# Stick-breaking layer of a two-block transformer kernel: normalisation after the product, additions in PSUM, results in two parts

## The chip, the cores and the metric

The kernel runs on one core of a Trainium2 chip. The metric is the device time of one execution in microseconds. Engines are called PE (TensorE), DVE (VectorE), ACT (ScalarE), POOL (GpSimd) and SP (SyncE, which issues the loads of weights).

## The reference, cut to what matters

The program computes two blocks of two layers each, on 512 tokens (528 with 16 meta tokens in the second block) of width 1024. The change is to the mixer of the second block's odd layer: a product to q, k and v, stick-breaking attention with 16 heads of 64, a product back.

```python
def stick_breaking(q, k, v):                 # 128-query blocks
    for i in range(L // BLOCK):
        s, e = i * BLOCK, (i + 1) * BLOCK
        z = einsum('bqhd,bkhd->bhqk', q[:, s:e], k[:, :e]) * scale      # scale = 1/8
        mask = (arange(e)[None, :] < arange(s, e)[:, None])[None, None]
        log_1m = where(mask, log_sigmoid(-z), 0.0)
        rest = cumsum(log_1m, axis=3, reverse=True) - log_1m
        a = where(mask, exp(log_sigmoid(z) + rest), 0.0)
        outs.append(einsum('bhqk,bkhd->bqhd', a, v[:, :e]))

def odd_mixer(h, w_in, w_out):               # h is rmsnorm(h, norm_mix[1])
    q, k, v = split(h @ w_in, 3, axis=-1)
    return stick_breaking(heads(q), heads(k), heads(v)).reshape(Bsz, L, C_W) @ w_out
```

With softplus(z) = -log_sigmoid(-z), a weight is exp(z minus the sum of the softplus of all keys from this one on that the query may see).

## The kernel before, in words

Activations are held transposed, features on the 128 partitions and the 528 tokens along the free dimension. Every large product is made in three passes over operands split into a high part (`hi`, rounded to fp32r) and a low part (`lo`, the rest): hi by hi, hi by lo, lo by hi. Weights come in panels of 1 MB (`Panels`, line 208): SP loads a panel two ahead (line 233), ACT makes its high part (line 244), DVE its low part (line 252), into two buffers each.

The odd layer (`odd_layer`, line 1971) is a row of blocks of code; all engines meet at the end of each block.

1. `normed_parts` (line 1673): the tails of two buffers are cleared on POOL, then `norm_stage` (line 527) squares the eight chunks of `hT` on ACT, adds them up with one-column matmuls (line 564), takes the root, spreads 1/rms over the partitions with matmuls of a diagonal (line 570), multiplies on DVE (line 600), and splits the result into two parts.
2. `product_stage` (line 333) makes q and k in 16 tiles of 48 matmuls (`wide_tile`, line 312, two matmuls of 264 columns to each stationary matrix), then v in 20 tiles of 24 matmuls of 256 columns (`row_tile`, line 324). ACT and DVE take finished tiles by turns (line 1032).
3. `stick_stage` (line 1735). Keys are on the partitions, queries along the free dimension. Key block t needs the queries from 128t on, so a head has 528 + 400 + 272 + 144 + 16 = 1360 columns. The work is in steps of one head each, written as a loop of four heads a turn (`over_steps`), and each engine works on several heads at different stages in one step. For a new head PE makes scores key block by key block (`score`, line 1920) into two PSUM tiles, from which ACT copies them, scaled by 1/8, to `z` in SBUF (line 1818). DVE bounds a copy (line 1897), ACT takes Exp and Ln (lines 1830, 1832), DVE takes the larger of that and z (line 1872), masks it (line 1876), masks z (line 1880), ACT and POOL split the softplus in two parts (lines 1825, 1851). For the head before, PE adds up the softplus over the keys into one PSUM tile, `sums`, from the last key block to the first (`add_up`, line 1934): after each block DVE subtracts the sums so far from z (line 1890), and PE may go on only when that is done (`normed`). ACT takes Exp of the finished z (line 1811) and PE mixes v with it (line 1959). ACT and POOL also stage the two parts of q and k for every pair of heads (lines 1805 to 1844), and POOL the head's part of v (line 1857).
4. `split_stage` (line 683) splits the result `y` into two parts on ACT (line 690) and DVE (line 697).
5. `product_stage` makes the product back, 8 tiles of 48 matmuls, which DVE adds to `hT` (line 1648).

The feed-forward layers (`ffn_layer`, line 2108) already do without step 1. `Parts` (line 2082) splits `hT` times the gain in two parts; `Rstd` (line 2010) works out 1/rms at the same time (squares on ACT, sums on POOL, two groups of small matmuls), and the tiles are multiplied by it as they leave PSUM.

## Time and profile before

| | |
|---|---|
| time, median of 3 runs | 3418.18 us (3412.99 to 3421.04) |
| time of the profiled execution | 3412.95 us |
| its span, first to last instruction | 3411.2 us |
| PE busy | 2788.7 us (82%) |
| DVE, ACT, POOL busy | 1237.9, 1033.5, 499.4 us |
| mean granted clock of PE | 0.796 of full speed |

The span is 1.75 us less than the time of the same execution. Stages follow one another with little overlap, so a stage's stretch of the span is its share of the time. "Busy" of PE says that matmuls were in flight, at either of its two clocks.

### The profile page before, as it was taken

Reading aid. Unit: us, or ns where it says so; the run is one execution under the profiler, and the core shown is the slowest. Engines: PE = TensorE matmul, PEld = TensorE weight load, DVE = VectorE, ACT = ScalarE, POOL = GpSimd, SP = SyncE. Lnnn points to the kernel's source line nnn. Section 1 sums busy time; section 2 is a strip of 40 time slices with the busy share of each in tenths; the row PEclk is TensorE's granted clock in tenths of the full one; section 3 lists DMA queues with packets and bytes.
Section 4 is the critical chain, followed back from the end, with each engine's and each line's share of the span. In section 5 each row is a group of like instructions: output and inputs, shape, how many; then the busy total and the mean of one; then the engine's idle time right before and its main releaser. Section 6 shows DMA issues by size and latency. Waiting matters only on the chain. (4 is left out here: it accounts for less than half of the span.)

```text
span 3411.2 us, 45824 instructions
## 1 busy us (share of the span) xinstructions
PE 2788.7 (82%) x18417; PEld 2577.8 (76%) x18417; DVE 1237.9 (36%) x2097; ACT 1033.5 (30%) x1535; POOL 499.4 (15%) x369
## 2 busy tenths in 40 slices
PE   5984978895697796669658989999896777799998
PEld 4973758894577696569447989999895554799998
DVE  1236232325423323331642344342323444343442
ACT  3233332225232210221323243231214444232232
POOL 0002100001100101200123033030002222032130
PEclk6996557897557698779555799999896666899998
DMA  3210001220001121011000223332220000232321
GB/s 105 87 50 6 1 3 50 87 75 6 1 1 52 38 75 42 19 50 56 33 1 0 68 75 84 97 91 77 71 79 1 0 0 0 62 83 77 105 74 59
DMA packets 232723, 165.44 MB, mean 48 GB/s; under 512 B 7439, under 2 KB 229513, under 8 KB 232421
## 3 DMA queue, kind: packets, MB, share of 16 engines
q1 hardware_dynamic: 232548, 162.91, 16.0%
q8 instruction: 134, 2.20, 0.3%
q14 instruction: 41, 0.33, 0.0%
HBM read 160.76 MB, written 2.14 MB: 48 GB/s over the span
## 5 line engine op out<-in xcount | busy, mean ns | idle before, releaser
L252 DVE TENSOR_TENSOR panel_lo<-panel_raw,panel_hi 128x2048 fp32r<-128x2048 f32 (+2 forms) x155 | 335.1, 2162 | 361.6 <-ACT panel_hi L244 361.6
L244 ACT ACTIVATE panel_hi<-panel_raw 128x2048 fp32r<-128x2048 f32 (+2 forms) x155 | 276.4, 1783 | 597.1 <-PE product L319 464.7
L328 PE MATMUL product<-panel_hi,normed_hi 128*128 128x256 f32 (+1 forms) x1336 | 378.7, 283 | 10.2 <-PEq L541 10.2
L328 PE MATMUL product<-panel_hi,normed_lo 128*128 128x256 f32 (+1 forms) x1336 | 378.6, 283 | 0.0
L328 PE MATMUL product<-panel_lo,normed_hi 128*128 128x256 f32 (+1 forms) x1336 | 378.6, 283 | 0.0
L319 PE MATMUL product<-scaled_hi,panel_hi 128*128 128x264 f32 x1408 | 289.9, 287 | 19.6 <-DVE scaled_lo L2097 12.5
L319 PE MATMUL product<-scaled_lo,panel_hi 128*128 128x264 f32 x1408 | 289.7, 287 | 0.0
L319 PE MATMUL product<-scaled_hi,panel_lo 128*128 128x264 f32 x1408 | 289.5, 287 | 0.0
L328 PEld LDWEIGHTS product<-panel_hi,normed_hi 128*128 128x128 f32 x1336 | 258.1, 193 | 10.2 <-issue 10.2
L328 PEld LDWEIGHTS product<-panel_hi,normed_lo 128*128 128x128 f32 x1336 | 258.2, 193 | 0.0
L328 PEld LDWEIGHTS product<-panel_lo,normed_hi 128*128 128x128 f32 x1336 | 258.1, 193 | 0.0
L319 PEld LDWEIGHTS product<-scaled_hi,panel_hi 128*128 128x128 f32 x1408 | 221.9, 191 | 20.9 <-DVE panel_lo L252 18.8
L319 PEld LDWEIGHTS product<-scaled_lo,panel_hi 128*128 128x128 f32 x1408 | 221.1, 191 | 0.0
L319 PEld LDWEIGHTS product<-scaled_hi,panel_lo 128*128 128x128 f32 x1408 | 220.9, 191 | 0.0
L319 PE MATMUL product<-normed_hi,panel_hi 128*128 128x264 f32 (+1 forms) x720 | 148.8, 288 | 40.2 <-PEq L541 40.2
L902 PE MATMUL scores<-panel_hi 64*128 64x512 f32 (+2 forms) x176 | 96.6, 670 | 93.8 <-POOL panel_lo L861 84.8
L564 PE MATMUL sums<-ones,squares 128*128 128x1 f32 x560 | 115.5, 343 | 63.5 <-ACT squares L549 63.5
L564 PEld LDWEIGHTS sums<-ones,squares 128*128 128x128 f32 x560 | 114.8, 319 | 66.1 <-ACT squares L549 66.1
L933 PE MATMUL mixed<-rows,e_turned 128*128 x768 | 151.3, 369 | 0.0
L933 PEld LDWEIGHTS mixed<-rows,e_turned 128*128 128x128 f32 x768 | 150.3, 291 | 0.1
L319 PE MATMUL product<-normed_lo,panel_hi 128*128 128x264 f32 (+1 forms) x720 | 148.1, 288 | 0.0
L319 PE MATMUL product<-normed_hi,panel_lo 128*128 128x264 f32 (+1 forms) x720 | 147.9, 287 | 0.0
(278 smaller groups left out, 5508.2 us busy)
## 6 DMA issues: line engine op xcount, KB each, us to landing
panel_raw<-in_w_in_dram SPq DMA_DIRECT2D x26, 1024.0 KB, 5.3
panel_raw<-in_ffn_w_gate_dram SPq DMA_DIRECT2D x44, 512.0 KB, 4.0
panel_raw<-in_ffn_w_up_dram SPq DMA_DIRECT2D x44, 512.0 KB, 5.3
panel_raw<-in_ffn_w_down_dram SPq DMA_DIRECT2D x32, 704.0 KB, 4.6
panel_raw<-in_even_w_in_dram SPq DMA_DIRECT2D x21, 1024.0 KB, 5.2
panel_raw<-in_odd_w_in_dram SPq DMA_DIRECT2D x12, 1024.0 KB, 5.1
panel_raw<-in_w_out_dram SPq DMA_DIRECT2D x8, 1024.0 KB, 5.1
panel_raw<-in_even_w_out_dram SPq DMA_DIRECT2D x8, 768.0 KB, 4.8
```

Source lines behind the costliest of these rows:

```text
L244: act.activation(c.hi[g % 2][:, 0:used], c.raw[g % 2][:, 0:used], ACT.Copy).then_inc(c.hi_made.sem, 1)
L252: dve.tensor_tensor(c.lo[g % 2][:, 0:used], c.raw[g % 2][:, 0:used], c.hi[g % 2][:, 0:used].bitcast(F32), ALU.subtract).then_inc(c.lo_made ...
L319: done = pe.matmul(out[:, b, 0:v - u], weight(w, k), a[:, k, u:v], start=(k == 0 and x == 0), stop=(k == chunks - 1 and x == 2))
L328: done = pe.matmul(out[:, 0, 0:v - u], a[:, k, t * P:(t + 1) * P], w[:, k, u:v], start=(k == 0 and x == 0), stop=(k == chunks - 1 and x == 2))
L564: done = pe.matmul(sums[:, t:t + 1], squares[k % 2][:, t * P:(t + 1) * P], c.ones[:, 0:1], start=(k == 0 and t == 0), stop=(k == KD - 1), ...
L902: done = pe.matmul(scores[a % s_ring][:, u:v], q[j][rows, b * P:(b + 1) * P], k[j][rows, u:v], start=(w == 0), stop=(w == 2))
L933: done = pe.matmul(mixed[n % 2][:, 0:d_v], e_turned[n % 2][0:rows, t, :], v_of(i, j, m, t)[0:rows], start=(t == 0), stop=(t == tiles - 1))
```

## The change

- The odd layer no longer calls `normed_parts`. A new block `odd_into` uses `Parts` and `Rstd`, makes v first (ACT multiplies a tile by 1/rms of its rows as it copies it), then q and k by turns; DVE multiplies their tiles by the spread 1/rms, ACT and POOL write the two parts, of all heads, to `q_hi`, `q_lo`, `k_hi`, `k_lo`. There is no staging for each head any more.
- A last block of fewer than 128 tokens is now one of 128 that begins at 400 (`block_starts`), so nothing is padded or cleared, in `Rstd` of the feed-forward layers too.
- In the new `stick_stage` z stays in PSUM, in three banks, for two heads at a time. PE makes the scores and adds the mask to them, by a matmul of the identity with the mask. Softplus is taken from it, and PE then adds minus 8 times its sums to the same banks. For each key block that takes the blocks after it too, so there is no running `sums` tile and no subtraction on DVE. ACT takes Exp from PSUM with scale 1/8.
- A head is handled in two parts (bank 0, 512 columns; banks 1 and 2, 864 columns), all written out without a loop. One activation table is loaded at the start of the stage.
- DVE writes the mixed values straight into `q_hi` and `q_lo`, from which the product back reads. `split_stage` is gone.

Core of the diff (constants, counters and signatures are left out):

```diff
-    into = Product(c, KD, 256, [Segment(8, columns(w_in, 0, 256), T_tiles(), take_into(lambda: cell.qk)),
-                             Segment(4, columns(w_in, 2048, 256), N_tiles(NB2), take_rows_into(lambda: cell.v))])
+    into = Product(c, KD, 256, [Segment(4, columns(w_in, 2048, 256), [("N", u) for u in block_starts(TOK)], None),
+                                Segment(8, load_qk, T_tiles(), None)])
...
+                for i in range(n_v):
+                    w_hi, w_lo = panels.split(pe, first + i)
+                    for t, at in enumerate(starts):
+                        n = i * len(starts) + t
+                        if n == RING:
+                            norm.pe_sums(pe, sums)
+                            norm.pe_spread(pe, sums)
+                        pe.wait_ge(c.v_taken.sem, c.v_taken.at(n - RING + 1))
+                        row_tile(...)
...
+                act.preload_act_table_set("natural_log_exp_and_others")
...
+                for h in range(H + 1):
+                    if h < H:
+                        x = soft[h % 2]
+                        for part in range(2):
+                            act.wait_ge(c.z_bounded.sem, c.z_bounded.at(2 * h + part + 1))
+                            act.activation(Stick.of(x, part), Stick.of(x, part), ACT.Exp).then_inc(c.z_exp.sem, 1)
+                        for part in range(2):
+                            act.wait_ge(c.z_exp.sem, c.z_exp.at(2 * h + part + 1))
+                            act.activation(Stick.of(x, part), Stick.of(x, part), ACT.Ln, bias=c.ones[:, 0:1]).then_inc(c.z_log.sem, 1)
+                    if h >= 1:
+                        for part in range(2):
+                            act.wait_ge(c.rest_ready.sem, c.rest_ready.at(2 * (h - 1) + part + 1))
+                            act.activation(Stick.of(weight[(h - 1) % 2], part), Stick.banks(z[(h - 1) % 2], part), ACT.Exp,
+                                           scale=0.125).then_inc(c.stick_made.sem, 1)
+                    if h < H:
+                        for part in range(2):
+                            act.wait_ge(c.plus_made.sem, c.plus_made.at(2 * h + part + 1))
+                            act.activation(Stick.of(plus_hi[h % 2], part), Stick.of(x, part), ACT.Copy).then_inc(c.plus_hi.sem, 1)
...
+                for h in range(H):
+                    add_up(h)
+                    if h >= 1:
+                        mix(h - 1)
+                    if h + 2 < H:
+                        score(h + 2)
+                mix(H - 1)
...
-            stick_stage(c, cell.qk, cell.v, y)
-        with ExitStack() as stage:
-            parts = [c.sb(f"y_{n}", [P, KD, TOK], F32R, into=stage) for n in ("hi", "lo")]
-            split_stage(c, y, KD, parts, out)
-            product_stage(c, out, parts, split, 2, solo=True)
+        q, k = ([c.sb(f"{name}_{part}", [P, KD, TOK], F32R, into=layer) for part in ("hi", "lo")] for name in ("q", "k"))
+        v = c.sb("v", [P, NB2, D], into=layer)
+        odd_into(c, into, q, k, v)
+        stick_stage(c, q, k, v)
+        product_stage(c, out, q, token_split(False), 2, solo=True)
```

Before, PE in the stick stage, a part of one head's `add_up` with the next head's `score` in between (`softplus_hi` and `softplus_lo` are the two parts of the softplus, `keys_before` and `keys_on` the triangular matrices of ones):

```order
L1934 MATMUL stick_sums<-softplus_hi,keys_before 128x16 [waits normed]
L1934 MATMUL stick_sums<-softplus_lo,keys_before 128x16
L1934 MATMUL stick_sums<-softplus_hi,keys_on 128x144
L1934 MATMUL stick_sums<-softplus_lo,keys_on 128x144
L1920 MATMUL stick_scores<-panel_hi 128x272 [waits logits_made]
L1920 MATMUL stick_scores<-panel_lo,panel_hi 128x272
L1920 MATMUL stick_scores<-panel_hi,panel_lo 128x272
L1934 MATMUL stick_sums<-softplus_hi,keys_before 128x144 [waits normed]
L1934 MATMUL stick_sums<-softplus_lo,keys_before 128x144
L1934 MATMUL stick_sums<-softplus_hi,keys_on 128x272
```

There are five such waits on DVE (`normed`) and five on ACT (`logits_made`) in a head. Now, PE at the same place, first the start of `add_up` (`stick_z` is z in PSUM, `stick_never` the mask, `stick_eye` the identity):

```order
L2036 MATMUL stick_z<-plus_hi,stick_keys_on 128x512 [waits plus_hi,plus_lo_dve]
L2036 MATMUL stick_z<-plus_lo,stick_keys_on 128x512
L2036 MATMUL stick_z<-plus_hi,stick_keys_all 128x400 [waits plus_lo_pool]
L2036 MATMUL stick_z<-plus_lo,stick_keys_all 128x400
L2036 MATMUL stick_z<-plus_hi,stick_keys_all 128x272
L2036 MATMUL stick_z<-plus_lo,stick_keys_all 128x272
```

and, 26 matmuls on, `mix` of the head before and `score` of the next but one:

```order
L2053 MATMUL stick_mixed<-stick,v 64x16 [waits y_lo,stick_made]
L2053 MATMUL stick_mixed<-stick,v 64x248
L2053 MATMUL stick_mixed<-stick,v 64x136
L2053 MATMUL stick_mixed<-stick,v 64x8
L2053 MATMUL stick_mixed<-stick,v 64x264 x3
L2053 MATMUL stick_mixed<-stick,v 64x144
L2053 MATMUL stick_mixed<-stick,v 64x16
L2011 MATMUL stick_z<-q_hi,k_hi 128x512 [waits stick_made]
L2011 MATMUL stick_z<-q_hi,k_lo 128x512
L2011 MATMUL stick_z<-q_lo,k_hi 128x512
L2016 MATMUL stick_z<-stick_never,stick_eye 128x112
L2011 MATMUL stick_z<-q_hi,k_hi 128x400 [waits stick_made]
```

PE now stops for others at five places in a head, and the 32 matmuls of an `add_up` stand together. ACT in the stick stage before, one head's turn:

```order
L1825 ACTIVATE softplus_hi<-softplus 128x1360 [waits turned]
L1828 REGISTER_ALU
L1830 ACTIVATE soft<-soft 128x1360 [waits masked]
L1831 REGISTER_ALU
L1832 ACT_TABLE_LOAD
L1832 ACTIVATE soft<-soft,ones 128x1360 [waits act_step]
L1809 REGISTER_ALU
L1810 REGISTER_ALU [waits normed]
L1811 ACT_TABLE_LOAD
L1811 ACTIVATE stick<-z 128x1360 [waits mixed]
```

and now, all of one head's turn:

```order
L1946 ACTIVATE soft<-soft 128x512 [waits z_bounded]
L1946 ACTIVATE soft<-soft 128x864 [waits z_bounded]
L1949 ACTIVATE soft<-soft,ones 128x512 [waits z_exp]
L1949 ACTIVATE soft<-soft,ones 128x864 [waits z_exp]
L1953 ACTIVATE stick<-stick_z 128x512 [waits rest_ready]
L1953 ACTIVATE stick<-stick_z 128x864 [waits rest_ready]
L1958 ACTIVATE plus_hi<-soft 128x512 [waits plus_made]
L1958 ACTIVATE plus_hi<-soft 128x864 [waits plus_made]
```

The two table loads of a head and its five copies of scores are gone, and the Exp of the head before stands between Ln and the high part of the new one.

## Rows read from the trace of the kernel before

**Rows 1.** The stick stage and the product before it, busy time of each engine
```profile
core 0: us, PE busy (x) PEld busy (x) DVE busy (x) ACT busy (x) POOL busy (x), PEclk, DMA share, GB/s
2420.00:2567.00 147.00, 147.00 (x1221) 147.00 (x1220) 32.62 (x28) 27.78 (x28) 0.00 (x0) 1.00 0.25 80
...
2573.00:2912.00 339.00, 236.65 (x808) 168.36 (x809) 155.03 (x318) 164.54 (x191) 85.28 (x48) 0.63 0.00 0
```
**Rows 2.** Timeline, ends and starts of the odd layer's stages: start us, duration us
```profile
2381.26 0.70 DVE L2220 TENSOR_TENSOR hT<-hT,product 128x528 f32<-128x528 f32 x1 [7.31 <-PE product L319]
...
2416.20 0.78 PE L319 MATMUL product<-normed_hi,panel_hi 128*128 128x264 f32 x2 [10.17 <-PEq L541]
...
2568.71 0.42 DVE L1032 COPY v<-product 128x256 f32<-128x256 f32 x1 [5.21 <-PE product L328]
...
2574.98 0.76 PE L1920 MATMUL stick_scores<-panel_hi 64*128 64x512 f32 x1 [6.31 <-POOL panel_lo L1844]
...
2913.69 0.78 DVE L1903 COPY y<-stick_mixed 64x512 f32<-64x512 f32 x2 [2.80 <-PE stick_mixed L1959]
...
2924.47 0.78 PE L319 MATMUL product<-y_hi,panel_hi 128*128 128x264 f32 x2 [10.81 <-PEq L685]
...
2973.72 0.70 DVE L1648 TENSOR_TENSOR hT<-hT,product 128x528 f32<-128x528 f32 x1 [5.17 <-PE product L319]
```
**Rows 3.** Groups of the stick stage: busy us, mean ns, idle before and its releaser
```profile
L1934 PEld LDWEIGHTS stick_sums<-softplus_hi,keys_before 128*128 128x128 f32 x64 | 17.9, 280 | 99.9 <-DVE z L1890 94.2 <-issue 3.5
```
**Rows 4.** Timeline of PE at the end of the stick stage, full clock
```profile
2902.07 0.28 PE L1934 MATMUL stick_sums<-softplus_lo,keys_before 128*128 128x144 f32 x1
2902.19 0.33 PE L1934 MATMUL stick_sums<-softplus_hi,keys_on 128*128 128x272 f32 x1
...
2903.17 0.40 PE L1934 MATMUL stick_sums<-softplus_hi,keys_before 128*128 128x272 f32 x1 [0.53 <-DVE z L1890]
2903.40 0.29 PE L1934 MATMUL stick_sums<-softplus_lo,keys_before 128*128 128x272 f32 x1
2903.53 0.35 PE L1934 MATMUL stick_sums<-softplus_hi,keys_on 128*128 128x400 f32 x1
2903.71 0.35 PE L1934 MATMUL stick_sums<-softplus_lo,keys_on 128*128 128x400 f32 x1
...
2911.04 2.61 PE L1959 MATMUL stick_mixed<-stick,v_head 128*64 128x512 f32 x12 [0.95 <-DVE y L1903]
```
**Rows 5.** Timeline of PE in the middle of the stick stage, low clock
```profile
2833.68 0.41 PE L1920 MATMUL stick_scores<-panel_lo,panel_hi 64*128 64x144 f32 x1
2833.89 0.41 PE L1920 MATMUL stick_scores<-panel_hi,panel_lo 64*128 64x144 f32 x1
2834.23 0.59 PE L1934 MATMUL stick_sums<-softplus_hi,keys_before 128*128 128x272 f32 x1
2834.62 0.43 PE L1934 MATMUL stick_sums<-softplus_lo,keys_before 128*128 128x272 f32 x1
2834.85 0.54 PE L1934 MATMUL stick_sums<-softplus_hi,keys_on 128*128 128x400 f32 x1
```
**Rows 6.** Granted clock of PE just after Rows 5, in stretches of 2 us
```profile
2838.00:2840.00 2.00, 2.00 (x4) 0.71 (x4) 1.46 (x3) 0.00 (x0) 2.00 (x1) 0.50 0.00 0
2840.00:2842.00 2.00, 2.00 (x12) 1.20 (x11) 1.86 (x1) 0.11 (x1) 2.00 (x2) 0.96 0.00 0
```
**Rows 7.** Groups of ACT, DVE and POOL in the stick stage
```profile
L1811 ACT ACTIVATE stick<-z 128x1360 f32<-128x1360 f32 x16 | 21.4, 1337 | 17.3 <-DVE z L1890 17.1
L1872 DVE TENSOR_TENSOR softplus<-soft,z 128x1360 f32<-128x1360 f32 x16 | 25.2, 1575 | 48.9 <-ACT soft L1832 48.9
L1851 POOL TENSOR_TENSOR softplus_lo<-softplus,softplus_hi 128x1360 fp32r<-128x1360 f32 x16 | 49.6, 3100 | 192.1 <-ACT softplus_hi L1825 192.1
```
**Rows 8.** Timeline, start of the second feed-forward layer (`Parts` and `Rstd`)
```profile
2974.78 1.91 ACT L244 ACTIVATE panel_hi<-panel_raw 128x2048 fp32r<-128x2048 f32 x1 [22.57 <-PEq L353]
...
2995.39 0.27 ACT L2052 ACTIVATE root<-product,eps 128x5 f32<-128x5 f32 x1 [0.53 <-PE product L2045]
...
2996.31 1.07 DVE L2059 TENSOR_SCALAR diagonal<-square,rstd 128x128 f32<-128x128 f32 x5
```

491 lines of the change are left out of this document (267 added, 224 removed).

## The prediction

> **What bounds the kernel now.** I read the busy shares first, then the odd layer's stages as stretches of the timeline, then the stick stage's waits, and last single matmuls at both clocks. The layer runs from the end of the layer before it (2381.96 us) to its own last addition (2974.42) [rows 2]: 592.5 us of 3411.2. It has four stretches. The normalisation holds PE's product back until 2416.20, 34 us. The product runs to 2568.7; PE is busy all the time at full clock [rows 1]. The stick stage takes 339.5 us from its first score (2574.98) to its last copy (2914.47), and there PE is busy only 236.65 of 339 us at a mean clock of 0.63 [rows 1, 2]: no engine is full (DVE 155, ACT 165 us). What bounds it is a round: PE adds the sums of one key block, DVE subtracts them, PE may go on. The first of these waits alone shows as 99.9 us of idle time, 94.2 of them released by DVE's subtraction [rows 3]. The idle stretches also cost the clock. So the stage is bound by handovers, and by the low clock that they bring. Last come 10 us of splitting (2914.47 to 2924.47) and 50 us of product.
>
> **The change part by part**, against the profiled execution, 3412.95 us.
>
> *Normalisation.* `odd_into` starts as the feed-forward layer does. There ACT starts 0.36 us after the last addition (2974.42 to 2974.78) and the root is made at 2995.39, 20.6 us later; the diagonals are done at 2997.38, 22.6 us after the start [rows 2, 8]. Here the start is 2382.3. PE makes three tiles of v meanwhile, then must wait for the sums and the spread: 22.6 us, plus about 2 for the spreading matmuls, 0.6 for ACT's copy of it and 0.4 for ACT's first v tile. It resumes at about 2407.9, with 3 tiles of 24 matmuls done. Before, 16 x 48 + 20 x 24 = 1248 matmuls took 152.5 us, 0.122 each, so three tiles are 8.8 us and the rest takes 143.7, to 2551.6. Before, PE was done at 2568.7. Gain 17. This is a stall that moves: instead of 34 us without a product there are some 7 us after the third tile, in which nothing else runs on PE. Bounds: 12, if ACT's queue (squares, panel, table load, root) is later behind the POOL sums; 20, if PE does not cool down.
>
> *Leaving and entering.* The last tile passes DVE (0.7), ACT (0.6) and POOL (about 1.4), to 2554.4; the stick stage then loads its table and makes its constants (about 2.3 us) and starts scores at 2557.1. Before: 2574.98, since it had a clearing block, q and k to stage on ACT, and POOL. Total gain so far 17.9 us. The staging of every pair goes from the stick stage; the same 32 splits now lie beside q and k tiles of 5.9 us each (528 columns: POOL 1.2, ACT 0.5, DVE 0.6 a tile [rows 7]), hidden; without that cover they would cost POOL's 19 us. The 12 loads on SP's queue are the same in another order, with 11 us or more between them. The clearing of a tail in the feed-forward layers costs POOL 0.2 us that nobody waits for: 0.
>
> *Stick stage, PE.* In PSUM form DVE's subtraction, the masking, the copies of scores, the zero matmul and two table loads a head are gone. PE gets more: 18 score matmuls (3 each of 512, 400, 272, 144, 32, 16 columns), 6 for the mask, 32 for the sums (2, 4, 6, 8, 10, 2 of 512, 400, 272, 144, 16, 32 columns), and 9 pieces to mix instead of 6. At full clock the starts are 0.18 us apart at 400 columns, 0.13 at 272, 0.12 at 144 [rows 4]; 512 by its columns 0.23; I take 0.115 for the shortest, which have a stationary matrix of the same size to load. That is 5 x 0.23 + 7 x 0.18 + 9 x 0.13 + 35 x 0.115 = 7.6 us. Mixing took 2.61 [rows 4]; three pieces more, in two passes each, make it 2.9. The first matmul after a wait takes 0.1 more (0.23 against 0.13 [rows 4]); five waits, 0.5. **PE needs 11.0 us a head.** At the low clock: 0.23 for 272, 0.21 for 144 and less [rows 5], 400 and 512 by twice the figures above; 2.3 + 2.5 + 2.1 + 7.4 = 14.3, mixing 5.8 (twice), waits 0.8: about 21 us a head.
>
> *Stick stage, the others.* ACT makes 1360 columns in 1.34 us [rows 7]; in two parts, 1.5. Exp, Ln, weights and high part: 6.1 us a head. DVE at 1.16 ns a column and 0.15 for each second instruction: bound, maximum, 512 columns of low part and two passes over the mixed values (528 each), 1.75 + 1.75 + 0.6 + 1.4 = 5.5. POOL: 864 columns at 3.1/1360, 2.0. All under 11.0. The handover chain that could bind: high part done, POOL 2.0, the rest of the sums 3.8, second weight part 0.9, high part of the next head 1.5: 8.2, and about 0.6 for handovers. After `add_up` of a head PE has mixing and scores (2.9 + 3.5 us) before it needs the next high part, which comes 2.7 after: a cover of almost 4 us. So PE is the bound. Which clock it gets is the main question: matmuls such as these, with hardly a gap, ran at 0.50 and then brought the clock to 0.96 [rows 5, 6]. With PE never idle over 2 us I take the full clock.
>
> *Sum of the stage.* 16 x 11.0 = 176. Start and end: PE idles about 3 us before head 0's sums, 4 us more over POOL and weight waits of the first two and last heads, and 1.4 for the last copy: 9. It starts at the low clock: 3.5. Together 189 against 339.5: 151 gained. Bounds: 10.0 a head (173 in all) if short matmuls cost less than I take, 12.5 (213) if each group costs 0.3 at its start.
>
> *Split.* 10.0 us become one handover, 0.4: gain 9.6. The first panel's parts of the product back are made beside the last q and k tiles.
>
> Sum: 17.9 + 150.5 + 9.6 = 178. 3412.95 - 178 = **3235 us** for a profiled execution. The median of the runs before was 5 us over the profiled one, so I say **3237**. Tellable from no change by this measurement is about 0.2%, 7 us.
>
> **A rule against rows.** Short matmuls are over half of PE's sum outside mixing; the trace gives 0.12 us for them [rows 4]. The Trainium skill, "TensorE: Matmul & The Clock Gate", Back-to-back issue gap, gives about 81 ns for a pair of weight load and 128-column matmul. By that, 35 short ones would cost 1.2 us less a head, 19 us in all, and the time would be 3218; the trace differs.
>
> **Rivals.**
> 1. *The short matmuls are cheaper than 144 columns show* (0.08 us, below what the rows have): 35 x 0.035 x 16 = 19 less, 3218. For it: [rows 4] have no matmul of 16 or 32 columns inside a long run. Against: at the low clock 144 columns take 0.21, more than their columns (0.12), so the load of the stationary matrix sets it. Chance 0.06. The page of the skill just named points this way.
> 2. *The clock comes and goes.* If PE's waits in a head are long enough to lose the clock for a third of the time, a head costs 11.0 + 10/3 = 14.3, 53 us more: 3290. For it: the stage before never held it. Against: its idle time was 99.9 us at one wait of 16 heads, 6 us each [rows 3], and I see none over 2. Chance 0.12.
> 3. *The chain of ACT, DVE and POOL binds.* If operations from PSUM or handovers eat the 4 us of cover and 2 more, 16 x 2 = 32: 3269. Chance 0.06.
> 4. *Low clock throughout*: 21 us a head, 16 x 10 = 160 more: 3397. Chance 0.03. The same skill page, LDWEIGHTS, has 1/1.2 ns a column whatever the clock: by it short ones would stay near 0.12, the head at 17.7 and the time at 3344; the 0.21 measured [rows 5] says otherwise.
> 5. *Slower than before: stationary matrices that are not loaded ahead.* `score` alternates 64-row keys with the 128-row identity, `add_up` changes matrices every second matmul. A matmul whose matrix came late took 0.39 instead of 0.23 [rows 5]. If all 56 paid 0.16 more at the low clock, 9 us a head: 30 us a head, 304 more than forecast: 3541. It decides from 22 us a head on, 11 above my figure. Against: runs of the same kind do not pay it [rows 4, 5]. Chance 0.03; a fraction of it, ending within 0.2%, 0.01.
> 6. *The change does not do what it says*: the table loads could stay. The order has one at the stage's start and none inside; even two a head (2.6 us) leave ACT at 8.7 of 11. No cost.
>
> **How the numbers follow.** My forecast, 3237 with 3218 to 3266 by its bounds (stage 173 to 213, normalisation 12 to 20), has 0.69. With rivals 1, 2 and 3 that is 0.93. The range of 8 in 10 reaches over rival 3 to rival 2: 3212 to 3290. Faster by over 0.2%: the forecast and rivals 1 to 4, 0.96; within 0.2%, 0.01; slower, 0.03.
>
> **What would show it.** PE's product resumes about 25 us after the stage's start, having stopped some 7 us after three v tiles. Scores start near 2557. In the stick stage, mixing starts come 11 us apart, PE is over 90% busy, clock near 1.0; ACT is about 55% busy with no table load inside. No split; the product back starts 0.5 us after the last copy, and the layer ends near 2797. Wrong would be: a period over 12.5, a clock of 0.8 or less (rival 2), or PE idle for ACT's high part (rival 3).

## The result, and the profile after

The changed kernel takes 3315.89 us (median of 4 runs, 3306.95 to 3317.69), the kernel before it on the same chip 3415.59 (3412.94 to 3421.04): a ratio of 0.9703, 95% interval 0.9687 to 0.9719. It is faster, by 100 us; forecast were 178, and the time lies above the range. The profiled execution took 3316.57 us, with a span of 3314.7 against 3411.2. The odd layer runs from 2379.35 to 2875.65, 496.3 us against 592.5: all of the gain lies in it.

Three of its four stretches came out as forecast. The timeline, start and duration in us, at their borders, follows; these lines answer to [rows 2] and [rows 8]:

```profile
2378.65 0.70 DVE L2314 TENSOR_TENSOR hT<-hT,product 128x528 f32<-128x528 f32 x1 [7.30 <-PE product L341]
2379.71 1.91 ACT L261 ACTIVATE panel_hi<-panel_raw 128x2048 fp32r<-128x2048 f32 x1 [15.63 <-PEq L2233]
...
2406.06 0.58 PE L352 MATMUL product<-panel_hi,scaled_hi 128*128 128x256 f32 x1 [1.06 <-ACT v L1809]
...
2555.14 0.79 PE L2011 MATMUL stick_z<-q_hi,k_hi 64*128 64x512 f32 x1 [5.16 <-ACT stick_keys_all L1940]
...
2826.53 0.71 DVE L1972 TENSOR_TENSOR q_lo<-stick_mixed,q_hi 64x528 fp32r<-64x528 f32 x1
...
2827.71 0.48 PE L341 MATMUL product<-q_hi,panel_hi 128*128 128x264 f32 x2 [1.96 <-PEq L1934]
...
2874.95 0.70 DVE L1672 TENSOR_TENSOR hT<-hT,product 128x528 f32<-128x528 f32 x1 [5.17 <-PE product L341]
```

PE's product resumes 26.3 us after ACT's start (forecast 25.6), the scores start 175.4 us after it (174.8), and the product back starts 0.5 us after the last copy (0.5). What is left is the stick stage, 2555.14 to 2827.24: 272.1 us, against 339.5 before and 189 forecast. Its windows, with the busy time and number of instructions of PE, weight load, DVE, ACT and POOL, then the granted clock; these lines answer to [rows 1]:

```profile
core 0: us, PE busy (x) PEld busy (x) DVE busy (x) ACT busy (x) POOL busy (x), PEclk, DMA share, GB/s
2555.14:2827.24 272.10, 270.60 (x1184) 224.31 (x1184) 88.71 (x112) 92.74 (x128) 32.24 (x16) 0.67 0.00 1
2555.14:2600.00 44.86, 44.86 (x150) 36.49 (x151) 12.30 (x15) 16.08 (x22) 5.62 (x3) 0.50 0.00 1
...
2620.00:2720.00 100.00, 100.00 (x468) 82.72 (x467) 34.03 (x43) 35.33 (x49) 12.12 (x6) 0.73 0.00 1
```

The idle time of [rows 3] is gone: PE is busy 270.6 of 272.1 us. DVE, ACT and POOL are busy 88.7, 92.7 and 32.2 us (forecast 88, 98 and 32), all far below the span. Yet the clock is at the lower of its two levels (1.2 GHz, shown as 0.50; the other is 2.4 GHz, shown as 1.00) for the first 45 us, and then comes and goes. In stretches of 2 us, with PE busy in all of each:

```profile
2616.00:2618.00 2.00, 2.00 (x8) 1.36 (x7) 0.69 (x1) 1.35 (x3) 0.57 (x1) 0.50 0.00 0
2618.00:2620.00 2.00, 2.00 (x10) 1.43 (x9) 0.00 (x0) 0.00 (x0) 1.44 (x1) 0.82 0.00 0
...
2632.00:2634.00 2.00, 2.00 (x11) 1.35 (x9) 0.69 (x1) 0.63 (x1) 1.09 (x1) 1.00 0.00 0
2634.00:2636.00 2.00, 2.00 (x11) 1.60 (x11) 0.00 (x0) 0.00 (x0) 0.00 (x0) 0.94 0.00 0
2636.00:2638.00 2.00, 2.00 (x8) 1.78 (x8) 1.21 (x2) 0.11 (x1) 0.00 (x0) 0.50 0.00 0
```

So the question for the experiments is why a busy PE loses its clock.

### The profile page after: what moved, and what is told of

It reads as the page before. It is cut to its first block and busy times, and to the rows that moved or that the text cites. A ratio compares the mean times of both kernels' runs of the same rounds, so it can differ in the third digit from the quotient of the medians.

```text
span 3314.7 us, 45528 instructions
## 1 busy us (share of the span) xinstructions
PE 2807.2 (85%) x18715; PEld 2618.1 (79%) x18715; DVE 1161.0 (35%) x1877; ACT 969.5 (29%) x1482; POOL 472.3 (14%) x347
## 5 line engine op out<-in xcount | busy, mean ns | idle before, releaser
L341 PE MATMUL product<-scaled_hi,panel_hi 128*128 128x264 f32 x1664 | 341.3, 286 | 19.4 <-DVE scaled_lo L2191 12.3
L341 PE MATMUL product<-scaled_hi,panel_lo 128*128 128x264 f32 x1664 | 341.4, 287 | 0.0
L352 PE MATMUL product<-panel_hi,normed_hi 128*128 128x256 f32 (+1 forms) x1176 | 332.8, 283 | 10.2 <-PEq L565 10.2
L341 PE MATMUL product<-scaled_lo,panel_hi 128*128 128x264 f32 x1664 | 341.1, 286 | 0.0
L352 PE MATMUL product<-panel_hi,normed_lo 128*128 128x256 f32 (+1 forms) x1176 | 332.8, 283 | 0.0
L352 PE MATMUL product<-panel_lo,normed_hi 128*128 128x256 f32 (+1 forms) x1176 | 332.7, 283 | 0.0
L341 PEld LDWEIGHTS product<-scaled_hi,panel_hi 128*128 128x128 f32 x1664 | 261.7, 190 | 20.5 <-DVE panel_lo L269 18.8
L341 PE MATMUL product<-inner_hi,panel_lo 128*128 128x264 f32 x704 | 143.3, 285 | 0.0
L341 PE MATMUL product<-inner_lo,panel_hi 128*128 128x264 f32 x704 | 142.6, 284 | 0.0
L341 PE MATMUL product<-inner_hi,panel_hi 128*128 128x264 f32 x704 | 142.4, 284 | 0.0
```

Of the source, the lines that this page charges most:

```text
L341: done = pe.matmul(out[:, b, 0:v - u], weight(w, k), a[:, k, u:v], start=(k == 0 and x == 0), stop=(k == chunks - 1 and x == 2))
L352: done = pe.matmul(out[:, 0, 0:v - u], a[:, k, at:at + P], w[:, k, u:v], start=(k == 0 and x == 0), stop=(k == chunks - 1 and x == 2))
```

## The experiments

Eighteen kernels ran. Four theories came up, the last one late:

- **A**: short matmuls stream few columns for the time that they take, and so lose the clock.
- **B**: PE's short stops lose it.
- **C**: matmuls that use half of the array (scores on 64 rows, mixing on 64 columns) do not count in full towards the clock.
- **D**: a stationary matrix that takes another number of rows (its height) than the one before it is loaded late; the array stands, and that loses the clock.

Every edit is against the changed kernel unless another is named. The ratio is to the kernel before, measured beside it; "stage" is the stick stage, from its first score (from the extra products ahead of it in `e12`, `e14`, `e15`, `e16` and `e17`) to its last copy; the next column is the granted clock in it, and "changes" counts, per head, how often a matrix of 64 rows follows one of 128 on PE, or the other way round.

| kernel | us | ratio, 95% interval | stage | clock | changes |
|---|---|---|---|---|---|
| changed | 3315.9 | 0.9703 (0.9687 to 0.9719) | 272.1 | 0.67 | 12 |
| e1_wide_short | 3287.2 | 0.9632 (0.9604 to 0.966) | 238.2 | 0.83 | 12 |
| e2_full_array | 3226.5 | 0.9454 (0.9414 to 0.9493) | 191.3 | 0.89 | 0 |
| e3_mix_thin | 3312.9 | 0.9707 (0.9678 to 0.9736) | 264.3 | 0.63 | 12 |
| e4_mix_between | 3285.4 | 0.9626 (0.9598 to 0.9654) | 241.8 | 0.78 | 12 |
| e5_full_mix | 3283.6 | 0.9633 (0.9605 to 0.9661) | 233.7 | 0.83 | 12 |
| e6_full_score | 3230.7 | 0.9478 (0.945 to 0.9505) | 185.5 | 0.89 | 0 |
| e7_full_mix_between | 3357.5 | 0.985 (0.9821 to 0.9878) | 314.9 | 0.59 | 12 |
| e8_padded | 3302.3 | 0.9688 (0.966 to 0.9716) | 259.4 | 0.75 | 12 |
| e9_stacked | 3214.6 | 0.9425 (0.941 to 0.9441) | 166.7 | 0.92 | 0 |
| e10_stacked_full_mix | 3217.7 | 0.9433 (0.9418 to 0.9449) | 172.3 | 0.91 | 0 |
| e11_two_full | 3282.3 | 0.9622 (0.9603 to 0.9641) | 233.6 | 0.82 | 12 |
| e12_shifted | 3318.0 | 0.9715 (0.9685 to 0.9744) | 282.8 | 0.65 | 12 |
| e13_padded_data | 3307.4 | 0.9681 (0.9661 to 0.9701) | 262.6 | 0.74 | 12 |
| e14_no_stop | 3216.4 | 0.9412 (0.9396 to 0.9429) | 172.2 | 0.92 | 0 |
| e15_changed_no_stop | 3314.4 | 0.971 (0.9693 to 0.9727) | 263.1 | 0.71 | 12 |
| e16_full_between_shifted | 3361.7 | 0.9858 (0.9832 to 0.9885) | 314.9 | 0.60 | 12 |
| e17_between_shifted | 3285.9 | 0.9632 (0.9608 to 0.9657) | 242.3 | 0.80 | 12 |
| e18_even_rows | 3231.5 | 0.947 (0.9455 to 0.9486) | 186.7 | 0.89 | 2 |

### Short matmuls, half the array, or stops

`e1_wide_short` widens every short matmul of the scores and sums (which changes their values):

```diff
-                                out = z[h % 2][:, bank, place % 512:place % 512 + n]
+                                if n < LEAST:
+                                    wide_place, u, n = min(place % 512, 512 - LEAST), min(u, TOK - LEAST), LEAST
+                                else:
+                                    wide_place = place % 512
+                                out = z[h % 2][:, bank, wide_place:wide_place + n]
...
-                                done = pe.matmul(out[:, 0:edge], eye[:], barred, start=False, stop=False, skip_group_check=True)
+                                done = pe.matmul(out[:, 0:LEAST], eye[:], wide_never[:], start=False, stop=False, skip_group_check=True)
```

> The changed kernel with every matmul of fewer than 240 columns in the scores, the mask and the sums (35 of 56 in a head) widened to 240 columns; it leaves the right values out (mask and sums are added in wrong places), and the count of instructions, the waits and all other engines are as in the changed kernel. In the changed kernel PE is never idle in the stick stage and yet has a mean clock of 0.67 and a stage of 272 us. Theory A (the clock falls where matmuls are short, since the array then streams columns for only half of the time, the rest being the change of the stationary matrix): the clock of the stage goes to 0.95 or more, the stage to 190 us or a little less, the time to about 3235. Theory B (the clock falls at PE's stops for other engines, too short to see as idle): stops are as before, so clock about 0.67 and time 3316, within 10. Theory C (matmuls that use half of the array, scores on 64 rows and mixing into 64 columns, do not count): about 3316 as well.

Measured 3287.2, stage clock 0.83. More work in less time: that speaks against B and against C, by which nothing would move, and A explains only a part (it had 0.95 and 3235).

`e2_full_array` makes both operations full. Its scores are then those of two heads added up, and wrong:

```diff
                 def score(h):
-                    rows = slice(64 * (h % 2), 64 * (h % 2) + 64)
+                    rows = slice(0, P)
...
-                    pe.wait_ge(c.y_lo.sem, c.y_lo.at(h - 1))
-                    rows = slice(64 * (h % 2), 64 * (h % 2) + 64)
+                    pe.wait_ge(c.y_lo.sem, c.y_lo.at(h))
+                    rows = slice(0, P)
...
-                                done = pe.matmul(mixed[rows, half, u - HALF * half:w - HALF * half], v[:, t, 64 * h:64 * h + 64],
+                                done = pe.matmul(mixed[rows, half, u - HALF * half:w - HALF * half], v[:, t, 128 * (h // 2):128 * (h // 2) + 128],
```

> The changed kernel with scores over all 128 rows (both heads of a pair summed) and mixing with 128 stationary columns; it computes other values for scores and mixed rows, with the same columns, pieces and number of matmuls. Mixing waits for one more copy of DVE, which lies some 5 us back. Theory C (half-used arrays do not count for the clock): clock of the stage 0.9 or more, time under 3260. Theories A and B: clock 0.67, time 3316 within 10.

3226.5 us: the full clock is there, and the forecast stage of 189 us too (191.3). I took this for C, and that was an error: full rows in the scores do not only use more of the array, they also take the 64-row matrices out of the kernel.

`e3_mix_thin` streams less in the mixing and leaves out most of the mixed values, `e4_mix_between` puts its two halves behind the two parts of the sums:

```diff
-                                at = Stick.stored(t, u)
+                                at, w = Stick.stored(t, u), w if t == 0 else min(w, u + META)
```

> The changed kernel with the mixing matmuls of key blocks 1 to 4 cut to 16 columns or fewer (leaves out most of the mixed values); mixing streams 600 instead of 1360 columns. It is the only long dense part of a head. Theory A: there is nothing left that lifts the clock, so it stays at 0.50 for most of the stage (mean under 0.58); a head costs 14.3 us plus some 3 of mixing at the low clock, so the stage stays near 270 us in spite of less work, time 3300 to 3330. Theory B: the clock stays near 0.67 and the head gets 2 us shorter, time about 3285. Theory C: mixing counts for less anyway, clock 0.67 or more, time about 3285.

```diff
-                def add_up(h):
+                def add_up(h, after_part):
...
                         done.then_inc(c.rest_ready.sem, 1)
+                        after_part(part)
...
-                    add_up(h)
-                    if h >= 1:
-                        mix(h - 1)
+                    add_up(h, lambda part: mix(h - 1, (part,)) if h >= 1 else None)
```

> The changed kernel with the two halves of mixing put after the two parts of the sums, instead of both after the second; same work, same results. Theory A: the sparse stretches are cut, so the clock falls less often if the level depends on the density of each stretch; clock 0.72 to 0.95, time 3240 to 3300; if the mean density of a head is what counts, nothing moves (3316 within 10). Theory B: one more place with a wait, clock 0.67 or less, time 3316 or more.

With less to stream the time hardly moves, 3312.9, since the clock falls to 0.63; with another order of the same work it is 3285.4, with PE as busy as before. Both show that the clock follows what PE does and not whether it is busy.

### Which half of the full array

`e5_full_mix` has the two mixing edits of `e2_full_array` alone, `e6_full_score` its edit of `score` alone.

> Only the mixing takes a stationary operand of 128 columns (both heads of a pair) instead of 64, and writes 128 rows, of which each head's own 64 are read on: same instructions, same columns streamed, right outputs. Scores stay on 64 rows. Theory C (the clock counts how much of the array is at work): mixing is about a third of the streamed time of a head and the scores about another third; if both count alike, half of the gain of both together comes: stick stage near 232 us, clock 0.76 to 0.82, 3270 us (3255 to 3290). Theory A alone (short matmuls lose the clock, half arrays count fully): nothing changes, 3316. If only columns count, and not rows: 3226 to 3235.

> Only the scores contract over 128 rows (both heads of a pair, so wrong values); the mixing stays on 64 columns. Theory C: the other half of the gain, stick stage near 232 us, clock 0.76 to 0.82, 3270 us (3255 to 3290). If rows do not count and only columns do: 3316. If rows alone count: 3226 to 3235. This and the run with full mixing together tell which half of the array the clock misses.

The scores alone bring all of it (3230.7), the mixing alone 32 us (3283.6). The second lies in the range that C gave, the first far outside it. The halves do not add up as C expected; rows seemed to count, columns hardly. `e7_full_mix_between` has the edits of `e4_mix_between` and `e5_full_mix` together.

> Full-column mixing, and its two halves placed behind the two parts of the sums, outputs right. If the two effects are of one kind (the array's work averaged over time) they add up: 30 us from the placement and 45 us from the full columns bring it near 3240 (3228 to 3262), stick stage near 200 us, clock over 0.85. If placement only helped by breaking up a stretch of half-used array, it gives nothing on top of the full mixing: the same time as that run within 6 us.

3357.5 us, the slowest up to here and under neither head: two edits that gain 30 us each lose 42 together. Neither A nor C can say that. `e8_padded` gives two of the three score products 128 rows by padding q with zeros, on top of full mixing:

```diff
+                def pad(h):
+                    for i in range(1):
+                        own = slice(64 * (h % 2), 64 * (h % 2) + 64)
+                        done = dve.tensor_copy(q_pad[h % 2][i][own, :], q[i][own, h // 2, :])
+                    done.then_inc(c.padded.sem, 1)
...
-                                    pe.matmul(out, k[x][rows, h // 2, keys], q[y][rows, h // 2, u:u + n], start=not started,
+                                    own = rows if y else slice(0, P)
+                                    pe.matmul(out, k[x][own, h // 2, keys], q[1][rows, h // 2, u:u + n] if y else q_pad[h % 2][0][:, u:u + n], start=not started,
```

> Full-column mixing, and two of the three score passes contract over 128 rows, of which the other head's 64 are zeros on the streamed side (a copy of q made by DVE, one more DVE instruction of about 0.6 us a head); outputs right. If the clock counts rows that are in use whatever they hold: near the run with everything full, 3230 to 3248, clock 0.85 or more. If rows of zeros count for nothing (the clock follows switching in the array): like full mixing alone, 3270, within 6 us of it.

3302.3, under neither head of its expectation. `e11_two_full` has the same heights with real data on all rows and 64-column mixing, `e13_padded_data` is `e8_padded` with another head's q in place of the zeros:

```diff
                                 for x, y in ((0, 0), (1, 0), (0, 1)):
+                                    rows = half_rows if y else slice(0, P)
```

> As the kernel with wrong full scores, but the third product (q's second part) stays on 64 rows, as in the run with zero rows; so it differs from that run by the zeros alone (and by its 64-column mixing). If rows of zeros count for nothing, this is near the full scores: 3230 to 3255, clock 0.80 or more, and over 40 us below the run with zeros. If zeros count as data does and two of three passes simply do not suffice: 3290 to 3310.

```diff
-                        dve.tensor_tensor(q_pad[j][i][other, :], q[i][other, 0, :].bitcast(F32), q[i][other, 0, :].bitcast(F32),
-                                           ALU.subtract)
+                        dve.tensor_copy(q_pad[j][i][other, :], q[i][other, 0, :])
```

> The kernel with padded scores, instruction for instruction, but the 64 rows of the padding hold another head's q instead of zeros (so the scores are wrong). If the clock follows switching in the array and zeros switch nothing: the time falls from 3302 to 3230 to 3265. If only the shape of the instruction counts: 3302 within 8 us.

3282.3, under neither head, and 3307.4, as the second head had it. Zeros or data make no difference (3302.3 against 3307.4, the runs overlap), so a kernel that computes wrong scores may still be read for its time. Two full products of three help far less than three.

### A version with full scores

`e9_stacked` lays the two parts of a head's q, and of its k, into one tile of 128 rows. A score is then two products of 128 rows, q's halves being exchanged in the second:

```diff
-                        act.activation(home(n, 0), taken[n % TAKEN][:], ACT.Copy).then_inc(c.qk_hi.sem, 1)
+                        for e in range(2):
+                            done = act.activation(stacked(n, e)[64 * e:64 * e + 64], taken[n % TAKEN][64 * e:64 * e + 64, :], ACT.Copy)
+                        done.then_inc(c.qk_hi.sem, 1)
...
+                def rest(n):
+                    dve.wait_ge(c.qk_hi.sem, c.qk_hi.at(n + 1))
+                    for e in range(2):
+                        own, other = slice(64 * e, 64 * e + 64), slice(64 - 64 * e, 128 - 64 * e)
+                        done = dve.tensor_tensor(stacked(n, e)[other], taken[n % TAKEN][own, :], stacked(n, e)[own].bitcast(F32),
+                                                 ALU.subtract)
+                    done.then_inc(c.qk_lo.sem, 1)
...
+                def swap(h):
+                    for e in range(2):
+                        own, other = slice(64 * e, 64 * e + 64), slice(64 - 64 * e, 128 - 64 * e)
+                        done = dve.tensor_copy(q_swapped[h % 2][other, :], q[h % 2][own, h // 2, :])
+                    done.then_inc(c.swapped.sem, 1)
...
-                                for x, y in ((0, 0), (1, 0), (0, 1)):
-                                    pe.matmul(out, k[x][rows, h // 2, keys], q[y][rows, h // 2, u:u + n], start=not started,
+                                for right in (q[h % 2][:, h // 2, u:u + n], q_swapped[h % 2][:, u:u + n]):
+                                    pe.matmul(out, k[h % 2][:, h // 2, keys], right, start=not started,
```

> Scores with 128 rows at work, outputs right: q and k of a head are laid down as one tile whose one half of the rows holds the first part and whose other half the second, and a score is two products of 128 rows (the second with q's halves exchanged) instead of three of 64; DVE makes the second parts and the exchanged q (two copies of about 0.4 us a head). Mixing stays on 64 columns. Theory C (the clock counts the rows that work): high clock after the first 40 to 45 us as with wrong full scores, scores a third cheaper (3.3 to 2.3 us at full clock), period 9.4 us, stick stage 170 to 182 us, 3212 us (3200 to 3232). If the full clock there came from the wrong values and not from the rows: clock under 0.75 and 3290 or more. DVE has 5.5 + 0.8 us a head, ACT 5.8, so neither binds.

> The same, with mixing on 128 columns as well. Theory C: with the scores full the clock is already high, so 0 to -6 us against the run before, unless full mixing shortens the low start (then up to -15). It waits for one copy-out of DVE more (1.6 us at most once). A loss of more than 8 us would say that what the mixing does to the clock hangs on its place in time, as the run with full mixing between the sums (3357) suggested.

3214.6 us with the stage at 166.7, 101 us under the changed kernel: it leaves nothing out, and no other kernel here is tellably faster. A head takes 9.35 us, by its mixing starts:

```profile
2643.08 2.75 PE L2076 MATMUL stick_mixed<-stick,v 128*64 128x16 f32 x18
...
2652.43 2.75 PE L2076 MATMUL stick_mixed<-stick,v 128*64 128x16 f32 x18
```

The exchange costs DVE 2.6 us a head where 0.8 was expected. At the start of the stage, with POOL at rest, two such copies take 0.87 us; beside POOL's low part they take three times as long and end some 0.3 us after it. The timeline of DVE and POOL:

```profile
2554.38 0.87 DVE L1977 CAST stick_q<-q_hi 64x528 fp32r<-64x528 f32 x2 [0.32 <-PEq L1788]
...
2645.35 2.63 DVE L1977 CAST stick_q<-q_hi 64x528 fp32r<-64x528 f32 x2
...
2645.49 2.20 POOL L2019 TENSOR_TENSOR plus_lo<-soft,plus_hi 128x864 fp32r<-128x864 f32 x1 [7.17 <-ACT plus_hi L1970]
```

DVE is busy 122.9 us of 166.7 now, so it is still not the bound.

Full mixing on top (`e10_stacked_full_mix`, the mixing edits of `e2_full_array`) changes nothing that the runs can tell: 3217.7, both within 3208 to 3219.

### The start of the stage, and its place in time

`e12_shifted` puts twelve products ahead of the first scores; `e14_no_stop` (on `e9_stacked`) and `e15_changed_no_stop` fill PE's stop at the start of the stage with such products, 28 and 24 of them.

```diff
+                for _ in range(12):
+                    pe.matmul(z[0][:, 0, 0:512], k[0][:, 0, 0:P], q[0][:, 0, 0:512], start=True, stop=True, skip_group_check=True)
                 score(0)
```

> The changed kernel with twelve more products of 64+64 rows and 512 columns before the first scores (their result is overwritten): 5 us of work more, and everything behind it that much later. If the clock depends only on the mix of work, the time is 3316 + 5 = 3321 (3314 to 3328). If where the stretches of low work fall in time decides, or if full work ahead of the stage brings the high clock sooner, it is off by more than 10 us, either way.

```diff
                                   parts.hi, parts.lo, KD, split).then_inc(c.product_ready.sem, 1)
+                for _ in range(14):
+                    pe.matmul(sums[:, 0:512], parts.hi[:, 0, 0:P], parts.hi[:, 1, 0:512], start=True, stop=True, skip_group_check=True)
...
+                for _ in range(14):
+                    pe.matmul(z[0][:, 0, 0:512], k[0][:, 0, 0:P], q[0][:, 0, 0:512], start=True, stop=True, skip_group_check=True)
                 pe.wait_ge(c.stick_constants.sem, c.stick_constants.at(5))
```

> The kernel with stacked scores (3214.6), with 28 products of 128x128 and 512 columns put into PE's stop at the start of the stick stage (14 at the end of the stage before, 14 ahead of the wait for the constants); nothing reads what they write. They take 0.22 us each at full clock, 6 us in all, of which at most 1 to 2 us may push the start back. If the stop of 6.4 us is what brings the low clock of the first 30 us: that stretch runs at full clock and gives back 12 to 18 us: 3196 to 3204. If the low clock there comes from the start's own thin work: 3212 to 3218.

> The changed kernel (3316) with 24 such products in the stop. If the stop alone made the clock low for the first 45 us and the half-used array keeps it toggling afterwards: 8 to 20 us less, 3296 to 3308, with the first fall of the clock at some later head. If the stop is what upsets the whole stage: full clock throughout, 3235 to 3250. If half-used scores bring the clock down at once: 3314 to 3320.

Shifting gave 3318.0 (its runs lie between 3306 and 3328), nothing but its own 5 us at most. Filling the stop moved the first fall of the clock and gained nothing in either kernel (3216.4 and 3314.4). The windows of `e15_changed_no_stop`, same columns as above, are the plainest sign against B. PE is busy without a gap from 2560, the first score begins at 2560.73 at the full clock, and the clock falls some 4 us into the scores:

```profile
2560.00:2564.00 4.00, 4.00 (x19) 2.66 (x17) 0.69 (x1) 0.85 (x3) 0.00 (x0) 1.00 0.00 2
2564.00:2568.00 4.00, 4.00 (x15) 2.89 (x13) 1.06 (x1) 0.66 (x1) 0.00 (x0) 0.63 0.00 0
```

In `e14_no_stop`, without changes of height, the clock stays full through the first scores and falls at a real stop, PE's wait of 3.4 us for ACT:

```profile
2560.00:2565.00 5.00, 5.00 (x36) 4.68 (x36) 1.75 (x2) 1.29 (x2) 0.00 (x0) 1.00 0.00 0
2565.00:2570.00 5.00, 1.64 (x8) 1.02 (x7) 3.83 (x5) 3.22 (x5) 1.10 (x1) 0.82 0.00 0
2570.00:2595.00 25.00, 24.18 (x96) 21.84 (x96) 14.04 (x15) 11.55 (x16) 5.22 (x3) 0.50 0.00 1
```

`e16_full_between_shifted` and `e17_between_shifted` are `e7_full_mix_between` and `e4_mix_between` with the twelve products of `e12_shifted`.

> The kernel with full mixing between the sums (3357), twelve products of 512 columns ahead of its first scores, whose results are overwritten: 5 us of work. If the mix of work alone sets the clock's share: 3357 + 5 = 3362 (3354 to 3368). If where the clock's changes fall in the head's rhythm decides: off that by more than 15 us, likely downwards (3270 to 3345), since 3357 is the odd one.

> The kernel with mixing between the sums (3285), the same twelve products ahead. If the mix of work sets the clock: 3290 (3283 to 3297). If the phase decides: off by more than 10 us, likely upwards (3300 to 3340).

3361.7 and 3285.9: each kernel keeps its time, so the place in time does not decide. My guess that the 3357 was an accident of phase fell.

### The height of the matrices

The weight loads of the changed kernel, read again, showed the theory that was missing. The timeline of the weight load, at full clock, two of the six groups of a score:

```profile
2664.74 0.18 PEld L2011 LDWEIGHTS stick_z<-q_lo,k_hi 64*128 64x128 f32 x1
2665.29 0.19 PEld L2016 LDWEIGHTS stick_z<-stick_never,stick_eye 128*128 128x128 f32 x1 [0.37 <-issue]
2665.54 0.18 PEld L2011 LDWEIGHTS stick_z<-q_hi,k_hi 64*128 64x128 f32 x1
...
2665.83 0.18 PEld L2011 LDWEIGHTS stick_z<-q_lo,k_hi 64*128 64x128 f32 x1
2666.28 0.19 PEld L2016 LDWEIGHTS stick_z<-stick_never,stick_eye 128*128 128x128 f32 x1 [0.27 <-issue]
```

A matrix of the height of its predecessor is loaded while the matmul before still runs. The mask's `stick_eye` has 128 rows and comes after 64; it is loaded at 2665.29, when the matmul before it (2664.97 to 2665.36) is all but ended, and the 64-row matrix behind it is late in the same way. All the kernels so far with a stage clock of 0.83 or less have twelve such changes a head, all with 0.89 or more have none: theory D. In `e8_padded`, `e11_two_full` and `e13_padded_data` the third product on 64 rows had put them back.

The place of the falls fits. Read in stretches of 1 us, the changed kernel's clock falls twelve times between 2600 and 2820, each time 2.7 to 5.8 us after the first product of a score: inside the scores, or up to 0.9 us behind them. It never falls in the mixing or later in the sums. The nine falls of `e7_full_mix_between` between 2600 and 2860 lie at 3.2 to 4.3 us. `e18_even_rows` keeps the scores on 64 rows and takes the mask's height down to them, which leaves half of the mask out. Two changes a head are left, into the scores and out of them:

```diff
-                                done = pe.matmul(out[:, 0:edge], eye[:], barred, start=False, stop=False, skip_group_check=True)
+                                done = pe.matmul(out[:, 0:edge], eye[rows], barred[rows], start=False, stop=False, skip_group_check=True)
```

> The changed kernel, scores on 64 rows as they are, but the mask's product takes the same 64 rows as the scores around it, so half of the mask is left out and the outputs are wrong. Theory C (rows at work): less of the array at work than in the changed kernel, so the clock is no better; 12 late matrices a head are gone, 1.3 to 1.7 us at full clock: 3280 to 3305, clock in the stick stage 0.60 to 0.72. Theory D (changes of height: each leaves the array standing while a matrix is loaded late, and these pauses lose the clock): full clock after the first heads as with full scores, period 10.4 us, stick stage 185 to 200 us, 3228 to 3245, clock over 0.87.

3231.5 us, stage 186.7, clock 0.89, as D had it (3228 to 3245), and 48 us below the lower end of C. Fewer rows are at work than in the changed kernel, and the clock is full after the start. The whole stage, and 100 us of it:

```profile
2557.29:2743.95 186.66, 182.89 (x1184) 165.05 (x1184) 88.62 (x112) 92.76 (x128) 32.53 (x16) 0.89 0.00 1
...
2620.00:2720.00 100.00, 100.00 (x721) 90.96 (x721) 54.17 (x68) 56.44 (x79) 18.34 (x9) 1.00 0.00 1
```

The matmuls of one group, changed kernel first, then `e18_even_rows` (with the two products ahead), both at full clock (start, duration):

```profile
2664.97 0.39 PE L2011 MATMUL stick_z<-q_lo,k_hi 64*128 64x512 f32 x1
2665.29 0.32 PE L2016 MATMUL stick_z<-stick_never,stick_eye 128*128 128x112 f32 x1
2665.54 0.44 PE L2011 MATMUL stick_z<-q_hi,k_hi 64*128 64x400 f32 x1
```

```profile
2659.41 0.50 PE L2011 MATMUL stick_z<-q_hi,k_hi 64*128 64x512 f32 x1
2659.75 0.39 PE L2011 MATMUL stick_z<-q_hi,k_lo 64*128 64x512 f32 x1
2659.98 0.39 PE L2011 MATMUL stick_z<-q_lo,k_hi 64*128 64x512 f32 x1
2660.22 0.21 PE L2016 MATMUL stick_z<-stick_never,stick_eye 64*128 64x112 f32 x1
2660.27 0.40 PE L2011 MATMUL stick_z<-q_hi,k_hi 64*128 64x400 f32 x1
```

From the third product to the next group it is 0.57 us instead of 0.29, so 0.28 for two changes. The scores of a head take 4.93 us (2664.39 to the first sum at 2669.32) instead of 3.40 (2659.41 to 2662.81), for ten changes more. `e9_stacked` gains 17 us on top of this: it has two products where there were three, and a head of 9.35 us instead of 10.34.

## Why the prediction was wrong, point by point

- **Normalisation, entering, split**: right. The stage starts 175.4 us after ACT's first operation (forecast 174.8); the split is one handover of 0.5 us. Two sums of the forecast are off by a little: 2554.4 and 2.3 give 2556.7 and not 2557.1, and the idle terms 3, 4 and 1.4 give 8.4 and not 9.
- **ACT, DVE and POOL in the stick stage**: right within 6 us each (88.7, 92.7, 32.2 against 88, 98, 32). Rival 3, their chain, did not come: the trace lists no wait of PE between the stage's start and its last matmuls. Nor did rival 6; there is one table load, at the start.
- **PE at full clock, 11.0 us a head**: near for what it counted, and somewhat high. `e18_even_rows` takes 10.34 (mixing starts at 2656.73 and 2667.07), and its stage is 186.7 where I had 189. It is made of 3.40 of scores, 4.26 of sums (2662.81 to 2667.07) and 2.68 of mixing; I had 2.9 of mixing. The slow starts are there (0.34 us at the first product of a score instead of 0.23), but the 35 shortest matmuls come 0.10 apart in the mean, 3.56 us a head, where I had 0.115 each and 4.0. What I left out is the late matrices: 4.93 - 3.40 = 1.53 us a head, 24 us over 16 heads even at full clock. With them a head of the changed kernel has 11.9 us of work at full clock. Its 272.1 us are 17.0 a head.
- **"With PE never idle over 2 us I take the full clock"**: this is the step that failed. PE was indeed not idle, and the clock was 0.67, the low level for two thirds of the stage. The stage took 272.1 us, 83 over the forecast and 85 over the 186.7 of the kernel with even heights: 24 of these 85 are the late matrices themselves, the other 61 the clock that goes with them. What I had read for it, [rows 5, 6], was one stretch in which the clock rose behind matmuls with hardly a gap; it does not say that it stays.
- **Rival 5**, the matrices that are not loaded ahead, named the mechanism and its place (64-row keys beside the 128-row identity) but dismissed it, since "runs of the same kind do not pay it". Just so: runs of one kind do not, changes of kind do, 12 a head, not 56. The 0.39 us that it priced stands in [rows 5] right behind the one change of height there, from scores (64*128) to sums (128*128). And its price lay less in the late loads than in the clock, so the kernel was slower than my 3237, but not slower than the kernel before. **Rival 2** had the clock come and go and 3290 us; it took PE's waits for the cause and a third of the time for the share, where it was two thirds. The two were one rival, and I priced them apart.
- **The start**: 3.5 us were forecast for the low clock at first. It lasts 47 us in the changed kernel, 40 in `e18_even_rows`, and between 21 and 56 in the other kernels that enter the scores after PE's stop. That the stage of `e18_even_rows` still ends within 3 us of the forecast is luck: its heads are 0.7 us shorter than forecast, 11 us in all, which hides a start and end that cost about 9 us more.
- **Rivals 1 and 4**: short matmuls in a row, each with its own matrix, come 0.11 apart at full clock, and 0.05 to 0.08 behind a longer one, so that rival 1 held in part (0.10 in the mean, against its 0.08). By rival 4's figure of 21 us a head the low clock all the time would have given 3397; the measured stage lies between the two levels.

The Trainium skill, "TensorE: Matmul & The Clock Gate", Step-by-step, says that the weight load is pulled ahead of running matmuls when the row groups do not conflict or when it goes to the background buffer, and that the number of rows does not matter for its time. Within one height the trace agrees: a load lies beside the matmul before it. Across heights it does not happen here, with 0.27 and 0.37 us of standing weight load. The same page of the Trainium skill, A second HAM failure mode, has a clock that goes up and down because PE idles briefly and often between groups of matmuls as it cycles through PSUM banks. The trace agrees that the clock goes up and down (0.67 at 270.6 of 272.1 us busy), but the banks are not the cause here: `e18_even_rows` goes through the same banks at the full clock.

Four things stay open. Among the kernels with twelve changes the times run from 3282 to 3362, reproducibly and whatever the shift, and I have no rule for that: full mixing gains 32 us alone and loses 72 between the sums. The length of the low stretch at the start, up to 40 us even with even heights and PE busy, is not explained either. The shortest way to the gain, all products of a head's scores first and then all its masks on 128 rows, so that two changes a head are left, was not tried. And that the pauses themselves, and not the change of height as such, lower the clock is argued from the place of the falls, not shown; `e18_even_rows` takes both away at once.

## What to carry to other kernels

Keep matmuls of one contraction height together; a 128-row identity or mask among 64-row products is loaded late both going in and coming out, 0.14 us each time at full clock, and can cost the high clock on top. Read the weight load's own timeline: PE's busy time hides these pauses (100 of 100 us busy from 2620 at a clock of 0.73), and a PE that is busy all the time is no promise of the full clock. When a full-size variant repairs the clock, change one thing more before the size is given the credit, because it may have made operations equal as well as large.

## What the runs showed of the hardware

- A PE busy 270.6 of 272.1 us ran at a granted clock of 0.67, and the same number of matmuls with even heights at 0.89, with 1.00 over the 100 us from 2620.
- Zeros or data on the added rows: 3302.3 and 3307.4 us, no difference.
- In the kernels with even heights a real stop of PE (3.4 to 6.4 us) at the start of this stage is followed by 26 to 40 us at the low clock. In `e14_no_stop`, after a stop of 3.4 us, PE is busy 24.2 of 25 us in it; filling the first stop only moved this behind the next wait.
- Short fp32r matmuls in a row, each with its own matrix, start 0.11 us apart at the full clock (`e18_even_rows`) and 0.21 at the low one ([rows 5]).
- DVE's copy of 64 rows and 528 columns between SBUF tiles takes 0.44 us alone and 1.3 us while POOL works (`e9_stacked`). It reaches the other half of the partitions without an extra: within the same half it takes 0.43 (`e8_padded`).
